# Four samples' values in one call, expert activations in three parts, and sums of squares with ones stationary, in a decoder step on one core

## The reference, cut to what matters

```
u, c, b, q, k, v, qx, gates = split(rms_norm(x) @ w_in)          # D = 1024
qx     = rms_norm(qx per head of 128, q_norm)                    # 4 heads: needs sums of squares of qx
y_conv = b * causal_conv(c * u)
y_sb   = stick_breaking(q, k, v)       # 8 heads; samples use cache_k, cache_v through page_table
mk, mv = rms_norm(mem) @ w_mem_kv ;  y_x = cross_attend(qx, mk, mv)
         # samples use their own cache_mem_k, cache_mem_v (8 x 256 x 4 x 128)
x1  = x + sum_g sigmoid(gates_g) * (y_g @ w_branch_g) @ w_o
out = x1 + sum of top-2 of 32 experts, each (silu(h @ w1) * (h @ w3)) @ w2      # D_EXPERT = 512
```

## Time and profile before

| | |
|---|---|
| median of 3 runs | 1062.99 us (1061.84 to 1064.9) |
| profiled execution | 1065.04 us |
| its span | 1063.3 us |
| busy share of PE, DVE, ACT, POOL | 97%, 54%, 31%, 15% |
| granted clock of PE | 0.99 of full |
| read from the chip's memory | 278 MB |

### The profile page before, as it was taken

How to read it: one execution, slowest core, us unless ns; L and a number is a source line. 1 busy time by engine, 2 the same in 40 slices (tenths; PEclk the granted TensorE clock), 3 DMA queues, 4 the chain that set the end, 5 groups by cost and what they waited for, 6 DMA issues and landing times.

```text
span 1063.3 us, 16217 instructions
## 1 busy us (share of the span) xinstructions
PE 1029.1 (97%) x6618; PEld 693.1 (65%) x6618; DVE 577.6 (54%) x925; ACT 325.6 (31%) x471; POOL 162.3 (15%) x198
## 2 busy tenths in 40 slices
PE   8999999999988999999999999999999999999996
PEld 8999999989857877999776434434333344334432
DVE  5222265688757666443546655555455555455545
ACT  6322243156536544322355111111111111111111
POOL 0000000114414563000000211101111111111100
PEclk9999899999999999999999999999999999999999
DMA  5632231647752332651446999999999999999982
GB/s 203 258 99 87 73 100 46 227 157 258 236 180 91 103 110 69 231 199 63 164 182 226 425 426 425 426 427 427 425 426 426 429 425 425 426 428 426 425 370 81
DMA packets 52618, 282.64 MB, mean 266 GB/s; under 512 B 7846, under 2 KB 8118, under 8 KB 32072
## 3 DMA queue, kind: packets, MB, share of 16 engines
q1 hardware_dynamic: 42360, 254.26, 59.5%
q0 software_dynamic: 7392, 21.09, 6.2%
q10 hardware_dynamic: 2800, 6.36, 1.7%
HBM read 278.29 MB, written 7.51 MB: 269 GB/s over the span
## 4 chain that ended last, share of the span: by engine, by line
PE 87%; DVE 4%; DMA 2%; ACT 2%; issue 2%; POOL 1%; ACTq 0%; SPq 0%; DVEq 0%; POOLq 0%
PE acc_all L813 25%; PE acc_all L1381 21%; PE acc_all L1428 10%; PE acc_all L1403 7%; PE acc_all L780 5%; PE acc_all L959 5%; PE acc_all L1194 3%; PE acc_all L999 2%; DMA vals<-in_cache_mem_v 1%; PE acc_all L1066 1%; PE acc_all L1429 1%; POOL vals L657 1%; PE acc_all L889 1%; PE acc_all L888 1%; PE acc_all L890 1%
## 5 line engine op out<-in xcount | busy, mean ns | idle before, releaser
L813 PE MATMUL acc_all<-xn_hi,w_hi 128*128 128x260 f32 x832 | 171.4, 287 | 6.0 <-DVE gate_sb L2123 2.4
L813 PE MATMUL acc_all<-xn_hi,w_lo 128*128 128x260 f32 x832 | 168.1, 284 | 0.0
L813 PE MATMUL acc_all<-xn_lo,w_hi 128*128 128x260 f32 x832 | 167.7, 283 | 0.0
L2560 DVE TENSOR_TENSOR x<-x,acc_all 128x1024 f32<-128x1024 f32 x127 | 151.5, 1215 | 1.1 <-PE acc_all L1403 1.1
L813 PEld LDWEIGHTS acc_all<-xn_hi,w_hi 128*128 128x128 f32 x832 | 129.3, 190 | 12.5 <-issue 5.4
L813 PEld LDWEIGHTS acc_all<-xn_lo,w_hi 128*128 128x128 f32 x832 | 128.8, 189 | 0.0
L813 PEld LDWEIGHTS acc_all<-xn_hi,w_lo 128*128 128x128 f32 x832 | 128.8, 189 | 0.0
L737 POOL TENSOR_SCALAR spread<-tok_row,slots 128x512 fp32r<-128x512 f32 x32 | 50.2, 1570 | 370.1 <-PE acc_all L1403 370.1
L1960 DVE TENSOR_TENSOR w_lo<-w_raw,w_hi 128x1024 fp32r<-128x1024 f32 x52 | 63.4, 1221 | 68.6 <-ACT w_hi L1566 68.4
L1867 ACT ACTIVATE few<-acc_all,slots 8x512 f32<-8x512 f32 x64 | 43.5, 679 | 152.9 <-PE acc_all L1429 121.0
L1861 ACT ACTIVATE gate_h<-acc_all 128x256 f32<-128x256 f32 x32 | 12.3, 384 | 234.6 <-PE acc_all L780 234.6
(11 more groups left out here) (380 smaller groups left out, 1857.3 us busy)
## 6 DMA issues: line engine op xcount, KB each, us to landing
w_a<-in_w SPq DMA_DIRECT2D x44, 1024.0 KB, 18.1
w_b<-in_w SPq DMA_DIRECT2D x44, 1024.0 KB, 19.0
w_c<-in_w SPq DMA_DIRECT2D x40, 1024.0 KB, 18.6
w_raw<-in_w_in SPq DMA_DIRECT2D x52, 512.0 KB, 3.7
w_a<-in_w SPq DMA_DIRECT2D x11, 2048.0 KB, 19.1
w_b<-in_w SPq DMA_DIRECT2D x11, 2048.0 KB, 19.4
w_c<-in_w SPq DMA_DIRECT2D x10, 2048.0 KB, 19.9
w_br<-in_w_branch SPq DMA_DIRECT2D x24, 256.0 KB, 4.9
```

The costliest lines, as they stand in the source:

```text
L813: mm = pe.matmul(out[:, a, :], w[:, slot, k, :], x[:, k, a * HALF_TOK:(a + 1) * HALF_TOK], start=first, stop=last)
L2560: dve.tensor_tensor(x1[:, t, :], x1[:, t, :], bank(2 * pair, 2), ALU.add).then_inc(back_ok, 1)
```

## The change

- Sums of squares (m = 16): the column of squares was stationary (128 tokens a time) and one column of ones moved, 20 matmuls. Now 32 columns of ones are stationary, each head has its own strip of the array, and the squares move, 512 columns for the prompt and 8 for the samples, 8 matmuls. The result lies with the tokens along the free axis, so DVE copies it to `qx_sums`, PE turns it at m = 17 in five transposes (a new job, `JOB_QST`), and DVE scales it then.
- Values: `four_values` takes four samples in four strips; `vals` are four tiles, two of them in a new region "v" of 8192 bytes a partition. Memory values are done at points 11 and 15, with loads of four samples after the softmax of n = 2, and in n = 6 ahead of ACT's sigmoid. Cached values are done at h = 2 and h = 4, with the gathers of samples 0 to 3 behind the triangles of pair 0 and of 4 to 7 behind those of pair 1. DVE copies all four samples at once (`four_out`).
- Expert activation: `act_t` in three parts, chunk 0, chunk 1 and chunks 2 and 3, and `down` waits for each.
- The scratch for DMA descriptors is given as 8192 bytes, where it was the default 16384.

```diff
+ACT_PARTS = ((0, 1), (1, 2), (2, CW))
...
-                           ("t", 61824), ("misc", 6144)):
+                           ("t", 61824), ("misc", 6144), ("v", 8192)):
...
-        vals = place("vals", "x", 4096, [2, PAGES, W])
+        vals = [place(f"vals{s}", "xv"[s // 2], 4096 * (1 - s // 2 + s % 2), [PAGES, W]) for s in range(PER)]
...
+        qx_sums = place("qx_sums", "t", 24576, [TOK])
...
-                pool.wait_ge(val_used, NB + b - 1)
+                slot = b % PER
+                pool.wait_ge(val_used, 2 + b // PER)
                 for j in range(PAGES):
...
-                        out=vals[:, slot, j, :], out_offset=None, in_=io["cache_v"],
+                        out=vals[slot][:, j, :], out_offset=None, in_=io["cache_v"],
                         in_offset=bass.IndirectOffsetOnAxis(ap=page_row[:, b * PAGES + j:b * PAGES + j + 1], axis=0),
-                    ).then_inc(val_ld[slot], 16)
...
-                for b in ((0, 1), (2, 3, 4, 5), (6, 7), ())[pair]:
+                for b in (range(PER), range(PER, NB), (), ())[pair]:
...
-                    for tt in range(NT):
+                    for at, part, n in ((out, slice(0, SEQ), SEQ), (bank(5), slice(SEQ, TOK), NB)):
                         for h in range(XH):
-                            mm = pe.matmul(out[0:rows(tt), tt * XH + h:tt * XH + h + 1], qx_sq[:, h, tok(tt)],
-                                           ones[:, 0:1], start=True, stop=True)
+                            mm = pe.matmul(at[COLS * h:COLS * (h + 1), 0:n], ones[:, 0:COLS], qx_sq[:, h, part],
+                                           start=True, stop=True)
                     mm.then_inc(tp_ps, 1)
                     pe.wait_ge(xn_ok, NT + 3)
                 elif m in (17, 18):
+                    if m == 17:
+                        pe.wait_ge(tp_sb, JOB_QSS + 1)
+                        for tt in range(NT - 1):
+                            turn(bank(5)[:, tok(tt)], qx_sums[:, tok(tt)], P)
+                        turn(bank(4)[0:NB, 0:P], qx_sums[:, SEQ:TOK], P).then_inc(tp_ps, 1)
+                    else:
+                        pe.wait_ge(tp_sb, JOB_QST + 1)
                     turn_memory(2 * (m - 17))
                     turn_memory(2 * (m - 17) + 1)
...
-            def two_values(kind, b, weight):
-
-                for slot in range(2):
-                    pe.wait_ge((mval_ld if kind == 0 else val_ld)[slot], (16 if kind == 0 else 32) * (b // 2 + 1))
+            def four_values(kind, g, weight):
+
+                pe.wait_ge((mval_ld, val_ld)[kind], 16 * PER * (kind + 1) * (g + 1))
                 for j in range(2):
-                    for s in (b, b + 1):
-                        at = COLS * (s % PER)
-                        mm = pe.matmul(bank(5)[at:at + COLS, :], weight[:, j, s, :], vals[:, s % 2, j, :], start=(j == 0),
-                                       stop=(j == 1))
-                mm.then_inc(val_used, 2)
+                    for s in range(PER):
+                        mm = pe.matmul(bank(5)[COLS * s:COLS * (s + 1), :], weight[:, j, PER * g + s, :], vals[s][:, j, :],
+                                       start=(j == 0), stop=(j == 1))
+                mm.then_inc(val_used, 1)
...
-                pe.wait_ge(yg_sb, 4 * kind + 2 * g + 2)
+                pe.wait_ge(yg_sb, 2 * kind + g + 1)
...
-                if 11 <= p < 15:
+                if p == 11:
                     pe.wait_ge(pmt_sb, 1)
-                    if p >= 13:
-                        pe.wait_ge(yg_sb, p - 12)
-                    two_values(0, 2 * (p - 11), pm_t)
+                    four_values(0, 0, pm_t)
+                if p == 15:
+                    pe.wait_ge(yg_sb, 1)
+                    four_values(0, 1, pm_t)
...
-                elif h == 7:
+                if h == 7:
...
-                    two_values(1, 2 * (h - 2), a_s)
+                    four_values(1, h // 2 - 1, a_s)
...
-                    if n is not None and c % 2 == 0:
-                        pe.wait_ge(actt_ok, 2 * n + c // 2 + 1)
+                    if n is not None and c < len(ACT_PARTS):
+                        pe.wait_ge(actt_ok, 3 * n + c + 1)
...
-            def load_memory_values(b):
-
-                if b == 0:
+            def load_memory_values(g):
+
+                if g == 0:
                     act.wait_ge(mid_st, MID_STORES)
                 else:
-                    act.wait_ge(val_used, b)
-                for v in (b, b + 1):
-                    act.dma_start(vals[:, v % 2, :, :], io["cache_mem_v"][v].rearrange("(t p) c -> p t c", p=P)
-                                  ).then_inc(mval_ld[v % 2], 16)
+                    act.wait_ge(val_used, 1)
+                for s in range(PER):
+                    act.dma_start(vals[s][:, :, :], io["cache_mem_v"][PER * g + s].rearrange("(t p) c -> p t c", p=P)
+                                  ).then_inc(mval_ld, 16)
...
+                if n == 6:
+                    load_memory_values(1)
...
-                if n in (2, 5, 6):
-                    load_memory_values(max(0, 2 * (n - 4)))
-                if n == 6:
-                    load_memory_values(6)
+                if n == 2:
+                    load_memory_values(0)
...
                 if m == 16:
                     dve.wait_ge(tp_ps, JOB_QSS + 1)
-                    dve.wait_ge(dve_step, steps_done[0])
-                    out = job_out(JOB_QSS)
-                    link(dve.tensor_scalar(ss_qx[:, 0:full], out[:, 0:full], 1.0 / XD, EPS, ALU.mult, ALU.add))
-                    dve.tensor_scalar(ss_qx[0:NB, full:full + XH], out[0:NB, full:full + XH], 1.0 / XD, EPS, ALU.mult,
-                                      ALU.add).then_inc(tp_sb, 1)
-                    dve.wait_ge(tp_sb, JOB_QSS + 1)
-                    dve.sem_inc(ms_ok, 1)
+                    dve.tensor_copy(qx_sums[:, SEQ:TOK], bank(5)[:, 0:NB])
+                    dve.tensor_copy(qx_sums[:, 0:SEQ], job_out(JOB_QSS)).then_inc(tp_sb, 1)
                 elif m in (17, 18):
+                    if m == 17:
+                        dve.wait_ge(tp_ps, JOB_QST + 1)
+                        dve.wait_ge(dve_step, steps_done[0])
+                        link(dve.tensor_scalar(ss_qx[:, 0:full].rearrange("p (t h) -> p t h", h=XH),
+                                               job_out(JOB_QST).rearrange("p (t h x) -> p t h x", t=NT - 1, h=XH)[:, :, :, 0],
+                                               1.0 / XD, EPS, ALU.mult, ALU.add))
+                        dve.tensor_scalar(ss_qx[0:NB, full:full + XH], bank(4)[0:NB, 0:P:COLS], 1.0 / XD, EPS, ALU.mult,
+                                          ALU.add).then_inc(tp_sb, 1)
+                        dve.wait_ge(tp_sb, JOB_QST + 1)
+                        dve.sem_inc(ms_ok, 1)
                     for q in (2 * (m - 17), 2 * (m - 17) + 1):
                         n = JOB_MT + q
                         dve.wait_ge(tp_ps, n + 1)
...
-                dve.wait_ge(val_used, kind * NB + b + 2)
+            def four_out(kind, g):
+
+                dve.wait_ge(val_used, 2 * kind + g + 1)
                 if kind == 1:
-                    dve.wait_ge(yt_ps, b // PER + 1)
-                at = COLS * (b % PER)
-                dve.tensor_copy(y_four[b // PER][at:at + 2 * COLS, :], bank(5)[at:at + 2 * COLS, :]).then_inc(yg_sb, 1)
+                    dve.wait_ge(yt_ps, g + 1)
+                dve.tensor_copy(y_four[g][:, :], bank(5)).then_inc(yg_sb, 1)
...
-                if n >= 6:
-                    two_out(0, 2 + 4 * (n - 6))
+                if n == 6:
+                    four_out(0, 0)
...
-                if n in (5, 6):
-                    two_out(0, 4 * (n - 5))
+                if n == KD - 1:
+                    four_out(0, 1)
...
-                if h in (3, 5):
-                    two_out(1, 2 * (h - 2))
...
                 if h in (2, 4):
-                    two_out(1, 2 * (h - 2))
+                    four_out(1, h // 2 - 1)
...
-            def act_out(done):
+            def act_out(parts_done):
 
                 up = bank(6).rearrange("p (c t) -> p c t", c=CW)
-                for part in range(2):
-                    c = slice(2 * part, 2 * part + 2)
+                for part, (c0, c1) in enumerate(ACT_PARTS):
+                    c = slice(c0, c1)
                     dve.tensor_tensor(gate_h[:, c, :], gate_h[:, c, :], up[:, c, 0:CAP], ALU.mult).then_inc(half_ok, 1)
-                    dve.wait_ge(half_ok, done + part + 1)
+                    dve.wait_ge(half_ok, parts_done + part + 1)
                     dve.tensor_tensor(act_t[:, c, :], gate_h[:, c, :], up[:, c, CAP:P], ALU.mult).then_inc(actt_ok, 1)
...
-    nc = bacc.Bacc("TRN2", target_bir_lowering=False, num_devices=1)
+    nc = bacc.Bacc("TRN2", target_bir_lowering=False, num_devices=1, dynamic_dma_scratch_size=8192)
```

(4 more changed lines are left out.)

21 lines of the change are left out of this document (9 added, 12 removed).

## The result

The changed kernel takes 1039.34 us (median of 4 runs, 1038.94 to 1040.5), beside 1063.7 us for the kernel before in the same job; the ratio is 0.9774 with a 95% interval of 0.9757 to 0.9792. That is 24.4 us less, where 22.1 were forecast. The profiled execution took 1038.94 us, 26.1 us less than the one of before; its span is 1037.1.

A forecast was written before the change was run, and what follows sets the result against it. TensorE was taken to bound the kernel, with DMA a second limit in the expert loop. Gains of 4.6 + 9.9 + 3.8 + 3.8 = 22.1 us took the profiled 1065.04 to 1042.9, as median 1041; range 1037 to 1049.

The forecast's parts named there:

- Sums of squares: At m = 16, job and following chunk shrink from 12.66 to 8.1 us if the clock stays up: gain 4.6.
- The premise on four strips: Memory value calls: four strips work beside each other, so 16 passes take 1.8 us and four calls become two.
- The 21.63 us: Loop turn n = 6 before the change; without value calls and transfer waits it falls to 11.68, a gain of 9.95.
- four take 20.3 at that rate, done at 305.6: Second memory-value load: two 512 KB loads took 10.17 us, so four land 1 us before point 15 at 306.9.
- the rival of a late load: Second memory-value load: each load takes 6.2 us, TensorE waits 4 us at point 15, total 1045; chance 0.10.
- the bound of 4.3: Cached values: gain if the calls at h = 3 and h = 5 go and POOL's gathers cause no delay.
- The 4.2 of the working: Expert activation: the first part comes 0.13 us earlier in each of 32 experts, 4.2 us in all.
- the cap: Expert loop: last weights are 3.7 us early, so a larger TensorE gain would wait for DMA; 3.8 taken.
- no wait for weights: Denies the rival that DMA at 426 GB/s alone sets the expert loop: 1044.8 us, chance 0.12.
- no second stall of the 5 us kind: Denies the rival that eight gathers behind pair 0 hit DVE's products twice: 3.6 us, 1044.6 in all, chance 0.08.
- strips beside each other: Refutes the rival that four strips do not run in parallel in value calls and sums: 8.5 us, 1049.5, chance 0.03.
- no gather slowed by the scratch: Denies the rival that halved descriptor scratch serializes POOL's gathers: +48 us, 1089 in all, chance 0.02.

The follow-up runs named there:

- the two kernels with other orders: Changed kernel with each call's samples 0 and 1 before 2 and 3: 1038.95 us; changed kernel with the first sample's matmuls given twice: 1044.79 us.

## Why the prediction was right

The time lies in the range, 1.7 us below the forecast. Term by term, forecast and found in the profile:

- *Sums of squares*, 4.6 and 5.1. The mechanism is as forecast, clock included. The size was off where the 8-column passes were priced at 0.112 each: the job takes 1.04, near the lower bound of 0.9 that the text gave. The other profiles of the old order say 3.7 to 5.1, and in timed runs the part alone gives 5.9, with an interval of 3.2 to 6.5.
- *Memory values*, 9.9 and 10.2. n = 6 shrank to 11.85 us and the calls kept their length. The premise on four strips was right, and the two kernels with other orders show why it holds. The 21.63 us that the prediction took away held a call of 3.38 us, which it read without asking why; its excess is a fall of the clock behind the wait. Wrong was the step "four take 20.3 at that rate, done at 305.6", and with it the margin of 1 us: the load took 13.7 us and was 8.0 us early. The rate came from one transfer beside key gathers, query loads and weights; doubling it was too slow by half. The error had no price, but the rival of a late load rested on it with its chance of 0.10; even issued 8.5 us later the load was in time.
- *Cached values*, 3.8 and 4.5 to 4.7, above the bound of 4.3 that the text gave for no delay at all. POOL's delay was put at 0.5 and was 0.1 to 0.3. That it came out near is partly luck: with the 0.30 us that stand ahead of each gather the working's own rows give 354.2 and not 353.4, and the four gathers more then took 1.03, 0.95, 1.96 and 0.95 and not 1.44 each. The 5 us gather came back once and not twice, as forecast. The Trainium skill (SBUF — State Buffer, "Who interferes with whom") says that a DVE instruction with two SBUF inputs contends with a GpSimd instruction that reads SBUF. The gathers read page_row from SBUF, and the traces agree: in all profiles of these runs together, 139 gathers start well inside such an operation, and each ends 0.75 to 0.85 us behind the end of that operation; 279 gathers of keys or values start beside none and take 0.94 to 1.06. The same section says that in its own probe a tensor_tensor did not stall a DMA; here it stalls a gather, and the measurement decides. What stays open is why the fourth gather sometimes waits for more than one of them. It starts 0.02 to 0.03 us behind the first product in all 13 profiles that have it there; in eight it ends behind this product, after 2.26 us, and in five, those of before and after among them, only behind the whole row of four, after 5.0. In the changed kernel's profile the path runs over it, and it still costs only 0.1 us: from the chunk behind the loop to the gate of h = 3 it is 46.35 us with the 5.0 and 46.24 to 46.26 with the 2.26, where POOL then waits 3.25 us for ACT.
- *Expert activation*, 3.8 and 4.5 (31 periods of 0.14, and 0.13 ahead of the first down). The 4.2 of the working were right; the step that failed is the cap, "the weights are 3.7 us early". They were 6.6 us early, since the 30.4 us to landing count from 1002.34 and not from 1005.35, so a gain of 4.5 was never near it, and a cap was no reason to take 3.8. The direction is as forecast: 6.6 us became 4.6. It shrank by less than the gain since the last load landed 2.2 us earlier against the loop's start than before; what made it so was not tried.
- *The scratch*, 0 and 0, now measured by itself and at half the size again, within 1 to 2 us.

The sum of the parts found is 5.1 + 10.2 + 4.5 + 4.5 = 24.3. They are read from two single executions, 26.1 us apart; the difference has 0.5 us from ahead of the first edit and some 1.6 us behind the issue of the last store in it, which no edit explains. That 24.3 is also the 24.4 of the medians is in part luck, since one execution of the old order can differ from the next by 1.4 us at m = 16 alone. Sums and activation were also timed alone, 5.9 and 4.8 us. The two kinds of values were not: their 14.7 us are read from the chain, and the medians leave 13.7 for them together. The mechanisms of both were tried one by one (strips, load, gathers), but not what each is worth.

All rivals fell: no wait for weights, no late load, no second stall of the 5 us kind (one of 1 us came), strips beside each other, no gather slowed by the scratch.

## What to carry to other kernels

Matmuls in column strips cost as much as their longest strip, whatever the order: fill all four strips before you count passes. A wait for a reload that can only start when the same step's work is done costs its whole transfer; with room for the next batch in SBUF it cost nothing here, and is worth looking for first in the chain of waits. A transfer's time in one crowded stretch is no rate for another, and it counts from the start of its own issue, not from the end of the group's row. A wait of TensorE can cost more than its length: look at the granted clock of what follows. One profile of a clock fall is no proof: compare the runs' times and mean clocks with it.

## What the runs showed of the hardware that was not expected

- The strips of the array take work in any order: 16 passes given as two strips and then two more lasted 1.94 us, given round the four strips 1.92, and 4 passes more in one strip made it 3.62.
- The fall of the clock behind a row of matmuls with few moving columns is not the same in each execution. With 24 columns it was absent in one profile (a chunk of 5.95 us) and there in the next (7.48); with one column, job and chunk took 12.66, 12.58 and 11.22 us in three profiles. With the ones stationary and the data moving they took 6.98 in all nine. The mean granted clock of 25 runs of the kernel before went from 0.988 to 0.995, and their times from 1066 to 1061 us with it.
- A wait of TensorE for a transfer was followed by a stretch at the lower clock (0.56 from 296 to 299 us), and a call of 1.9 us took 3.38 to 3.63 in six profiles.
- A POOL gather that starts while DVE runs an operation with two SBUF inputs ends 0.75 to 0.85 us behind that operation (139 gathers), where it takes 0.94 to 1.06 otherwise; one that starts 0.01 us ahead of DVE took 0.95. One that starts 0.02 us behind the first of four in a row waits for the first (2.26 us, eight profiles) or for all four (5.0, five profiles).
- Four loads of 512 KB on ACT's queue landed 13.7 us after the first issue when that was at 279.4 us, and 11.6 us after it at 287.8, beside other traffic; two of them had taken 10.6 us before.
- Descriptor scratch of 16384 or 8192 bytes (the kernel before), and of 8192 or 4096 bytes with eight gathers of 256 KB in a row (the changed one), gives the same time within 0.2%.
